# Most of the modulation products move from TensorE to GpSimd, beside the later stages

## What is computed

```python
mod = (jax.nn.silu(c) @ w_ada[l] + b_ada[l]).reshape(B, N_MOD, D)      # 9 vectors of 1024
m = [mod[:, j] for j in range(N_MOD)]
h = modulate(rmsnorm(x, ffn1_pre_g[l]), m[0], m[1])
x = x + 0.5 * m[2][:, None, :] * rmsnorm(swiglu(h, ...), ffn1_post_g[l])
h = modulate(rmsnorm(x, mix_pre_g[l]), m[3], m[4])                      # mixer, gate m[5]
h = modulate(rmsnorm(x, ffn2_pre_g[l]), m[6], m[7])                     # second feed-forward, gate m[8]
...
mod_x = split(silu(c_2) @ ada_w[i] + ada_b[i], 6)                       # per layer i of the second block
mod_c = split(silu(c_ctx_2) @ ada_w[i] + ada_b[i], 6)                   # the same weights, second condition
```

## Time and profile before

| | us |
|---|---|
| median of 3 runs (4368.36 to 4372.31) | 4371.32 |
| span of the profiled execution | 4369.0 |
| TensorE busy | 3904.0 (89%) |
| VectorE busy | 2385.0 (55%) |
| ScalarE busy | 1631.1 (37%) |
| GpSimd busy | 649.4 (15%) |

### The profile page before, as it was taken

How to read it: one execution, slowest core, us unless ns; L and a number is a source line. 1 busy time by engine, 2 the same in 40 slices (tenths; PEclk the granted TensorE clock), 3 DMA queues, 4 the chain that set the end, 5 groups by cost and what they waited for, 6 DMA issues and landing times. The chain is left out here.

```text
span 4369.0 us, 60220 instructions
## 1 busy us (share of the span) xinstructions
PE 3904.0 (89%) x22780; PEld 3311.7 (76%) x22780; DVE 2385.0 (55%) x4520; ACT 1631.1 (37%) x1818; POOL 649.4 (15%) x265
## 2 busy tenths in 40 slices
PE   6889866897769899999998999999798898899999
PEld 2359765894457678888877888888576797899999
DVE  5765454541565379877840344444456598603655
ACT  5764331432233332444432222222323445443443
POOL 0000000000000035433333000000000283372000
PEclk9989986998889899999999999999899999999999
DMA  8975321441101234366664555555210455777776
GB/s 337 351 268 183 128 94 39 154 164 49 57 1 39 96 107 146 129 177 184 190 185 156 201 192 196 208 192 192 92 63 34 156 204 144 192 245 242 272 284 211
DMA packets 377067, 715.93 MB, mean 164 GB/s; under 512 B 213376, under 2 KB 265856, under 8 KB 315840
## 3 DMA queue, kind: packets, MB, share of 16 engines
q1 hardware_dynamic: 371840, 696.32, 46.7%
q10 hardware_dynamic: 4368, 13.15, 0.8%
q0 software_dynamic: 688, 4.19, 0.3%
HBM read 605.59 MB, written 108.00 MB: 163 GB/s over the span
## 5 line engine op out<-in xcount | busy, mean ns | idle before, releaser
L2056 POOL TENSOR_TENSOR arena_split<-ring,arena_split 128x1024 fp32r<-128x1024 f32 x256 | 646.5, 2531 | 3270.6 <-ACT arena_split L2014 3270.6
L2274 PE MATMUL ps<-arena_split 128*128 128x512 f32 (+1 forms) x6144 | 1071.8, 338 | 22.7 <-DVE arena_split L2258 22.7
L2274 PEld LDWEIGHTS ps<-arena_split 128*128 128x128 f32 x6144 | 951.0, 190 | 143.4 <-issue 21.1
L2076 PE MATMUL ps<-xT_split,arena_split 128*128 128x512 f32 (+1 forms) x4096 | 1022.5, 340 | 30.9 <-ACT arena L2023 17.7
L2076 PEld LDWEIGHTS ps<-xT_split,arena_split 128*128 128x128 f32 x4096 | 713.5, 192 | 111.3 <-issue 30.6
L266 DVE TENSOR_TENSOR arena_split<-ring,arena_split 128x2048 fp32r<-128x2048 f32 x204 | 466.1, 2292 | 516.3 <-ACT arena_split L260 513.8
L2076 PE MATMUL ps<-hT_split,arena_split 128*128 128x512 f32 (+1 forms) x2048 | 693.3, 339 | 0.0
L2255 DVE TENSOR_TENSOR arena_split<-ring,arena_split 128x2048 fp32r<-128x2048 f32 x128 | 293.4, 2292 | 513.9 <-ACT arena_split L2235 513.9
L260 ACT ACTIVATE arena_split<-ring 128x2048 fp32r<-128x2048 f32 x204 | 388.5, 1912 | 456.8 <-PE ps L662 156.1
L2235 ACT ACTIVATE arena_split<-ring 128x2048 fp32r<-128x2048 f32 x128 | 245.2, 1916 | 714.8 <-PE ps L2274 709.8
L2076 PEld LDWEIGHTS ps<-hT_split,arena_split 128*128 128x128 f32 x2048 | 393.6, 192 | 38.7
(11 more groups left out here) (242 smaller groups left out, 4405.8 us busy)
## 6 DMA issues: line engine op xcount, KB each, us to landing
ring<-in_weights SPq DMA_DIRECT2D x472, 1024.0 KB, 4.9
gates<-arena SPq DMA_DIRECT2D x48, 1024.0 KB, 6.9
activations<-arena SPq DMA_DIRECT2D x128, 256.0 KB, 2.1
arena<-gates SPq DMA_DIRECT2D x64, 512.0 KB, 5.9
arena<-activations SPq DMA_DIRECT2D x64, 512.0 KB, 6.7
activations<-arena SPq DMA_DIRECT2D x128, 128.0 KB, 2.3
arena<-gates SPq DMA_DIRECT2D x64, 256.0 KB, 5.0
arena<-activations SPq DMA_DIRECT2D x64, 256.0 KB, 5.2
```

The source lines that it names most:

```text
L2056: pool.tensor_tensor(low, self.raw(f)[:, j, :], high.bitcast(F32), ALU.subtract)\
L2076: mm = pe.matmul(k.ps[:, j, 0:self.T], self.u[:, 2 * (f % 2) + j, a, t * P:(t + 1) * P], self.h[b][:, t, :], start=n == 0, stop=n == 3 * D ...
L2274: mm = pe.matmul(k.ps[:, t, 0:self.T], self.v[:, f % 2, a, j * D + t * P:j * D + (t + 1) * P], self.weighted[:, f % 2, b, j, :], start=fir ...
```

## The change

- `MOD_HEAD = 8`: of the 84 modulation chunks only the first 8 (m[0] and m[1], what the first norm needs) stay in the ring and on TensorE. The ring is 76 chunks shorter (`SKIPPED`).
- A new object `SideModulation` lets GpSimd do the other 76. Its loop `accumulate` loads half a chunk (128x1024, 512 KB) by a transfer of its own into one of two buffers, multiplies each of the half's two 128x512 tiles by a condition value for each partition (`tensor_scalar`) and adds the products up (`tensor_tensor`). Two chunks make a *group* of 512 outputs. For `mod1` a group has one condition: per half two multiplies and two additions, 15 operations a group with one sum as result (14 groups). For `mod2` it has two conditions: 30 operations a group, two sums (24 groups). The sums are 62 in all.
- A sum is 128 partitions x 512; it is still to be added up over the partitions. `turn` does that on TensorE, four matmuls of one column for each sum, at fixed places: sums 0 to 7 at the start of the first `PostNorm`, 8 to 15 at the start of `Recurrence`, 16 to 23 in the second `PostNorm`, 24 to 31 in ffn2 between up and down, 32 to 37 in the third `PostNorm`, 38 to 61 in `PeerAdd` of layer 0. VectorE adds the bias and makes the gains there (`add`, `gains`).
- There are 8 buffers for sums (`KEPT`): GpSimd may begin sum n only when sum n-8 has been turned (`side_taken`). The last 24 sums (layer 1) have buffers of their own and are made in `PeerValues` of layer 0 (`before_second`).
- The bias table comes laid out from the host; ACT loads it (2 MB) in `Projections`. `Setup` waits for two loads instead of eight; ctxT, lru_w and w_rope are loaded later. `DiffLambda` goes behind the `Norm` of layer 1.

```diff
+MOD_HEAD = 8
+SKIPPED = N_MOD1 // 2 + N_MOD2 - MOD_HEAD
...
-        self.load = k.count_of("small_loads", 16 * 8)
+        self.load = k.count_of("small_loads", 16 * 2)
...
-        pe.wait_ge(self.load.sem, self.load.at(16 * 8))
-            mm = pe.matmul(k.ps[:, h, :], self.rel[:, h, :], self.onehot, start=True, stop=True)
...
+    def accumulate(self, pool, chunks, streams, buf, products, keep):
+        def load(i):
+            chunk, half = halves[i]
+            pool.dma_start(buf[:, i % 2, :], io["weights"][chunk, :, half * self.HALF:(half + 1) * self.HALF])\
+                .then_inc(self.loaded[i % 2].sem, 16)
...
+        for i in range(len(halves)):
+            pool.wait_ge(self.loaded[i % 2].sem, self.loaded[i % 2].at(16 * ((base + i) // 2 + 1)))
+            if quarter == 0 and keep and n + len(streams) > keep:
+                pool.wait_ge(self.taken.sem, self.taken.at(n + len(streams) - keep))
...
+                    self.after(pool, 1)
+                    pool.tensor_scalar(totals[j] if new else products[j], w[:, tile], k.cs[:, s * DT + t:s * DT + t + 1],
+                                       None, ALU.mult).then_inc(self.steps.sem, 1)
+                for j in range(2 * (not new)):
+                    self.after(pool, 1)
+                    pool.tensor_tensor(totals[j], totals[j], products[j], ALU.add).then_inc(self.steps.sem, 1)
+            if i + 2 < len(halves):
+                pool.wait_ge(self.steps.sem, self.steps.at(scaled))
+                load(i + 2)
...
+    def turn(self, pe, lo, hi, bank):
+        for n in range(lo, hi):
+            pe.wait_ge(self.steps.sem, self.steps.at(self.ready[n]))
+            for q in range(4):
+                mm = pe.matmul(k.ps[:, bank, at:at + 1], total[:, q // 2, q % 2 * P:(q % 2 + 1) * P], k.ones[:, 0:1],
+                               start=True, stop=True)
+            mm.then_inc(self.taken.sem, 1)
...
-            PostNorm(k, k.coef[:, 0, 1, :], at=after),
+            PostNorm(k, k.coef[:, 0, 1, :], after, turn(0, 8, blocks=[(0, 1), (1, 0), (1, 1)])),
-            Recurrence(k),
+            Recurrence(k, turn(8, 16, blocks=[(2, 0), (2, 1)])),
-            PostNorm(k, k.coef[:, 1, 1, :], at=k.mix.scratch),
+            PostNorm(k, k.coef[:, 1, 1, :], k.mix.scratch, turn(16, 24)),
-            FeedForward(k, "ffn2", h_ffn),
-            PostNorm(k, k.coef[:, 2, 1, :], at=after),
+            FeedForward(k, "ffn2", h_ffn, turn(24, 32, bank=0)),
+            PostNorm(k, k.coef[:, 2, 1, :], after, turn(32, 38, layer=0)),
```

416 lines of the change are left out of this document (258 added, 158 removed).

## The result

The changed kernel takes **4491.5 us** (median of 4 runs, 4490.45 to 4497.07) against 4371.23 for the kernel before, a ratio of 1.028, 95% interval 1.027 to 1.029: 2.8% slower. The forecast was 4324 us, and the range ended at 4440. The profiled span is 4489.3 us against 4369.0, so 120.3 us are to be found.

A forecast was written before the change was run, and what follows sets the result against it. Modulation was taken as DMA-bound, then TensorE sets the feed-forwards' pace. ffn1 237 us earlier shrinks through turns and waits to 65 ahead, less 2 and 16: 47 us off 4369 gives 4322 span, 4324 us; range 4225 to 4440.

The forecast's parts named there:

- The multiplication's price: GpSimd's multiply of 512 elements, absent from the trace: taken as 0.7 us, between 0.53 (memset) and 1.2 (addition).
- What VectorE takes from GpSimd: Whole time of VectorE's low parts, norm operations and hidden-row low parts added to GpSimd's work, as the ports lock exclusively.
- My walk: Turn-by-turn reckoning to the third PostNorm of when GpSimd's sums are ready and TensorE asks; new kernel 65 us ahead there.
- What GpSimd takes from VectorE: Short VectorE operations each wait for one GpSimd operation: 15 us in recurrence and indexer, 14 in a norm.
- the rest: TensorE's path to the third PostNorm's turn, without ffn1's start and the turns; only short VectorE waits were forecast to lengthen it.
- the second row: Trace evidence in the prediction: a VectorE operation of 0.3 us took 2.43 when GpSimd was first.
- the rule I quoted: Skill's rule: shared ports are an exclusive lock; two-input VectorE instructions contend with GpSimd ones that read SBUF.
- The turns: One-column matmuls before layer 0's PeerValues: eight sums 8 us, 2 us where TensorE waits; waits 0, 59, 0, 19, 52.
- Layer 1's turns: 24 sums in PeerAdd take 25 us, starting 2 us in; the sums of squares then end 16 us later.
- ffn1's start: First feed-forward starts at 66 us instead of 303, so 237 us ahead.
- PeerValues holds GpSimd's work: Layer 0's PeerValues: GpSimd's 374 us plus VectorE's 292 make 666 of 703 us, which barely fits.
- rival B: GpSimd becomes the bound through the multiply's price: no gain from 0.97 us, 4455 to 4510 us at 1.2; chance 0.25.

The follow-up runs named there:

- h_both_ts: Kernel with the host's bias table, GpSimd making only mod2 for both layers (24 chunks beside early stages, 24 in PeerValues), TensorE all of mod1: 4342.55 us.
- e_nomul: Changed kernel with multiplications left out except the first two of each group (52 of 304 stay), additions kept: 4364.53 us.
- e_tt: Changed kernel with GpSimd's products made by two-tensor operations, the condition value broadcast along the row: 4605.85 us, ratio 1.055.
- e_noadd: Changed kernel without the additions of GpSimd's sums, except the 14 joining halves of one-condition sums: 4282.89 us, ratio 0.981.
- e_memset: Changed kernel with all products and additions but each group's first replaced by memsets of about the same length, which read nothing: 4318.18 us, ratio 0.989.
- e_gap: The version with only two-tensor operations on GpSimd, plus an 8-column memset (0.10 us) behind each operation: 4562.7 us, ratio 1.045.

## Why the prediction was wrong

**The multiplication's price** is the step that failed first. I took 0.7 us, with 0.53 and 1.2 as ends, reasoning that one input is half of two. Measured: 1.55 us. The upper end, the addition's price, was no upper end. A turn's lateness is a sum of such operations, so this term carried into every wait of the walk. 304 multiplications before the third PostNorm at 0.85 us more are 258 us of GpSimd's time. The Trainium skill, "GPSIMD Engine Reference", section "4.1 Engine selection", calls one-input operations roughly line-rate; measured against the addition, the multiplication with a scalar for each partition is slower here, not faster, so the sentence that I drew on pointed the wrong way. The other prices were close: addition 1.25 (1.2), a load's issue 0.61 (0.8). A group with one condition is 23.7 us and not 17.2, one with two 45.0 and not 31.2.

**What VectorE takes from GpSimd** I set too high, and it covered part of the first error. My walk gave GpSimd 92 (with 10 in the head), 39, 26, 73 and 24 us of waiting, some 250. Measured up to 1054 us: the multiplications' sums, 489.5 + 75.8, less 304 at 1.56 make 91, the additions' 391.5 less 266 at 1.26 make 56: 147 us.

**What GpSimd takes from VectorE** I set too low: 15 us in Recurrence and the indexer and 14 in a norm, less 7 that came back, so +23 in the rest. Measured: +49, and 27 more that lay hidden in the wait before (from Recurrence's turn to the next took 194.7 us in h_both_ts and 167.3 in the changed kernel). The 27 us compare two kernels with different work on GpSimd and are an estimate. The price of one event, one operation of GpSimd, was right for many of them; that a series of additions can hold on longer, and that the form of both operations matters, was not in my account, although the second row was a tensor-scalar operation of VectorE already, and not the two-input one that the rule I quoted speaks of.

**The turns.** From TensorE's arrival to the last sum turned, the walk has 8, 61, 8, 21 and 54 us; measured are 18.6, 94.1, 19.5, 50.4 and 82.1. The waits for GpSimd were 8.7, 82.7, 9.7, 39.7 and 73.0 us, where I had 0, 59, 0, 19 and 52. The order is right and every size too small: 265 against 152 us for the turns. Eight sums that wait for nothing take 8.9 to 12.1 us and not 8.

**Layer 1's turns.** I had 25 us for 24 sums, 16 of them on the path; they took 41.0 us and moved the next PeerValues by 40.7. My price of 1.05 us came from one-column matmuls on two partitions, in a stretch at clock 0.97; these load 128x128 weights, at 1.2 GHz. Of what I had put down as unchanged, 7 us were lost by DiffLambda's new place, which I had not priced.

Of the 167 us between the foretold span (4322) and the measured one (4489.3), the turns' lengths are 113, the rest 26, layer 1 another 25 and ffn1's start 2.5. The multiplication's price stands behind the first: e_nomul, with 52 of the 304 multiplications left, has one wait of 5.9 us. How much of the 113 us the price alone makes is not shown, since GpSimd lost less to VectorE than I had put down, and that worked the other way.

**What was right.** ffn1's start. That PeerValues holds GpSimd's work: it did even with the dearer multiplication, where rival B feared up to 59 us more. GpSimd's last sum was ready at 3205.8 us, 26 after PeerValues' end, and no turn waited, as the earlier sums were turned meanwhile. Rival B named the mechanism, the places and the direction, and its rule, 18 us for each 0.1 us of the multiplication, gives 4477 us at 1.55, close to the measured time. That closeness is luck: the rule counts only the three turns that wait, and with sums 0-7 and 16-23 late as well, as B has them at 1.2 us, my walk comes to some 4560 us at 1.55, before anything for PeerValues, while the share of VectorE, which I had set some 100 us too high, works the other way. And B stopped at 1.2 us and had a chance of 0.25. The range was too narrow for the same reason: the bound for an operation that no row showed came from a belief about its inputs. One reading was wrong and cost nothing: GpSimd is empty in slices 23 to 31 of the earlier trace rows (and 38 to 40), not in 20 to 33.

## What to carry to other kernels

Before work is moved to GpSimd, measure the very form of instruction there: a form with fewer inputs can be the slower one, and an unseen price has no safe upper end in a neighbour's. Then ask two things of every stage beside which it will run: whether TensorE will ask for the result before it is ready, and whether VectorE is on the path there with short dependent operations. The second cost more than its share of busy time says, and making GpSimd faster made it worse. Put such work beside a stage in which VectorE has slack (here 24 chunks in PeerValues, 1.8% gained together with the host's table, which alone gave 0.5%) and leave the rest where it was. Even there the form counts: with two-tensor operations alone PeerValues took 22 us more.

## What the runs showed of the hardware

- GpSimd, 512 fp32 elements for each partition, alone: tensor times a scalar for each partition 1.55 us, tensor plus tensor 1.25, tensor times a broadcast column 1.03 to 1.05, a memset 0.53. Issuing a 512 KB load took it 0.53 us at least and 0.61 in the median (changed kernel).
- A series of two-tensor operations on GpSimd, back to back, held a 0.17 us operation of VectorE for 8.04 us, until GpSimd issued a load (e_tt); four additions in a row held a two-tensor one for 5.41 (e_nomul). MAX8 of VectorE, with one input, took 428 ns in the indexer before and after.
- One-tensor operations of GpSimd gave way instead: 1.83 us on average up to 1200 us, and the path's stages grew by 14 us only (e_noadd).
- Beside memsets on GpSimd VectorE's two-tensor operations kept their 0.48 us, and a tensor-scalar one of 0.41 took up to 1.77 (e_memset). Breaks of 0.10 us let VectorE's tensor-scalar operation in at the third and not at the first two (e_gap). Why stays open; so does why additions one at a time cost VectorE more than two in a row (+80 against +49 us).
- TensorE's granted clock was 0.51 in a stretch that came right behind 700 us at 1.00, once TensorE did only one-column matmuls: 333 ns for a weight load that took 186 to 192 at the higher level.
